# Contiguous 16 KB rows for the experts' down matrices, with a strided channel order in the up products

## The reference

```python
def expert_block(args):
    xb, e = args
    return (jax.nn.silu(xb @ w1[e]) * (xb @ w3[e])) @ w2[e]
```

## Time and profile before

| what | value |
|---|---|
| median of 3 runs | 2577.6 us (2574.97 to 2588.11) |
| the profiled execution | 2590.55 us, span 2588.7 us |
| PE busy | 2180.5 us, 84% of the span |
| VectorE, ScalarE, GpSimd busy | 27%, 18%, 8% |
| queue q1 | 101,632 packets, 496.34 MB, 49.0% of 16 engines over the span |
| queue q0 | 10,880 packets, 16.81 MB, 2.0% |
| packets in all | 112,871, of them 95,344 under 8 KB |
| expert matrices | 192 loads of 2 MB, median 27.5 us from issue to landing |

### The profile page before, as it was taken

The page is one execution under the profiler, slowest core; times in us unless marked ns, Lnnn a source line. Parts: engine busy times, 40 slices in busy tenths (PEclk is TensorE's granted clock), DMA queues, the critical chain, the costliest instruction groups (busy, mean ns, idle before and its releaser), DMA issues.

```text
span 2588.7 us, 32038 instructions
## 1 busy us (share of the span) xinstructions
PE 2180.5 (84%) x13514; PEld 1161.7 (45%) x13514; DVE 689.5 (27%) x1396; ACT 461.7 (18%) x1041; POOL 204.2 (8%) x240
## 2 busy tenths in 40 slices
PE   6899888867999888877778599999999788887773
PEld 3345788864645443222223344775554533222221
DVE  6203667664102221000001321452021310000003
ACT  3211344431102100000000100551021000000001
POOL 1000111101000011111111000000000111111110
PEclk9999899998999889898899799899999799889987
DMA  4020000011224559999998321001324599999994
GB/s 131 33 87 11 10 3 3 3 59 57 98 97 159 204 210 406 406 407 405 407 405 329 136 97 65 33 18 65 130 68 173 229 387 408 408 410 410 401 405 183
DMA packets 112871, 514.96 MB, mean 199 GB/s; under 512 B 20544, under 2 KB 21704, under 8 KB 95344
## 3 DMA queue, kind: packets, MB, share of 16 engines
q1 hardware_dynamic: 101632, 496.34, 49.0%
q0 software_dynamic: 10880, 16.81, 2.0%
q10 hardware_dynamic: 240, 0.07, 0.0%
HBM read 503.73 MB, written 28.31 MB: 206 GB/s over the span
## 4 chain that ended last, share of the span: by engine, by line
PE 64%; DMA 24%; DVE 7%; issue 2%; SPq 2%; ACT 1%; DVEq 0%; POOL 0%; ACTq 0%; POOLq 0%
DMA big<-in_moe_w 23%; PE ps L1510 17%; PE ps L1497 11%; PE ps L1846 8%; PE ps L1616 6%; PE ps L1865 4%; PE ps L1556 2%; PE ps L1717 1%; PE ps L1709 1%; SPq L453 1%; PE ps L1483 1%; PE ps L1770 1%; PE ps L1782 1%; PE ps L1872 1%; PE ps L1731 1%
## 5 line engine op out<-in xcount | busy, mean ns | idle before, releaser
L1846 PE MATMUL ps<-big 128*64 128x512 f32 x2048 | 510.0, 655 | 156.7 <-DMA big<-in_moe_w 156.4
L1510 PE MATMUL ps<-big 128*128 128x512 f32 x1024 | 440.6, 592 | 0.0
L1846 PEld LDWEIGHTS ps<-big 128*64 128x64 f32 x2048 | 176.7, 151 | 486.9 <-issue 486.9
L1510 PEld LDWEIGHTS ps<-big 128*128 128x128 f32 x1024 | 194.3, 190 | 242.7 <-issue 242.5
L1497 PE MATMUL ps<-big 128*128 128x512 f32 (+1 forms) x768 | 277.9, 524 | 6.6 <-issue 6.6
L1426 DVE SCALAR_TENSOR_TENSOR big<-big,ps 128x256 f32<-128x256 f32 x64 | 27.0, 422 | 891.3 <-ACT big L939 891.3
L1865 PE MATMUL ps<-big 128*64 128x512 f32 x1024 | 233.8, 598 | 30.7 <-ACT big L946 30.7
L1497 PEld LDWEIGHTS ps<-big 128*128 128x128 f32 x768 | 146.5, 191 | 136.1 <-issue 128.6
L1616 PE MATMUL ps<-big 64*64 64x64 f32 x5632 | 180.9, 221 | 8.0 <-DVE big L1125 5.5
L1616 PEld LDWEIGHTS ps<-big 64*64 64x64 f32 x5632 | 173.6, 137 | 15.8 <-issue 9.7
L946 ACT ACTIVATE big<-ps 128x256 f32<-128x256 f32 x64 | 24.6, 384 | 677.5 <-PE ps L1855 677.5
(11 more groups left out here) (296 smaller groups left out, 1968.6 us busy)
## 6 DMA issues: line engine op xcount, KB each, us to landing
big<-in_moe_w SPq DMA_DIRECT2D x192, 2048.0 KB, 27.5
big<-in_mx_wkv SPq DMA_DIRECT2D x8, 2048.0 KB, 7.9
big<-in_rw_wrkv SPq DMA_DIRECT2D x6, 2048.0 KB, 8.0
big<-in_mb_wqkv SPq DMA_DIRECT2D x6, 2048.0 KB, 8.0
big<-in_mx_wq SPq DMA_DIRECT2D x4, 2048.0 KB, 8.0
big<-in_mx_wo SPq DMA_DIRECT2D x4, 2048.0 KB, 8.0
h_rows<-big SPq DMA_DIRECT2D x4, 2048.0 KB, 10.3
big<-y_rows SPq DMA_DIRECT2D x8, 1024.0 KB, 8.0
```

The source lines that it names most:

```text
L1510: ins = mm(d[:], lhsT=lhs[:, k, t * P:(t + 1) * P], rhs=w[:, k, :], start=k == 0, stop=k == KT - 1)
L1846: ins = mm(ps[2 + b][half * BR:(half + 1) * BR, :], lhsT=hgT[b][:, k], rhs=w13[set_][:, :, k, half * 256:(half + 1) * 256], start=k == 0, ...
```

## The change

Two lines. The down matrix is now read as `(p k) n`: partition p takes the consecutive rows 4 p to 4 p + 3, one run of 16 KB, as the up matrices do. Group f of `w2` then holds the inner channels 4 p + f rather than 128 f + p. So that the columns of `hT` fit these, the up products take their moving columns in another order. Inner channel 4 q + 2 a + b, with a the half, lands in half a, in column 128 b + q. Within `w13` the neighbours of a moving row are then 4 floats, 16 bytes, apart: 128 of them for b = 0, 128 for b = 1, the same again for the second matrix. The number of instructions, waits and bytes stays on every engine and in every queue, and so does their order.

```diff
             def down_matrix(l, b, e):
-                src = moe_w2[l].rearrange("e (k p) n -> e p k n", p=P)[bass.ds(e, 1)]
+                src = moe_w2[l].rearrange("e (p k) n -> e p k n", p=P)[bass.ds(e, 1)]
                 sp.dma_start(w2[b], src.rearrange("o p k n -> (o p) k n")).then_inc(e_w[l][3 * b + 2], 16)
...
                         for half in range(2):
                             ins = mm(ps[2 + b][half * BR:(half + 1) * BR, :], lhsT=hgT[b][:, k],
-                                     rhs=w13[set_][:, :, k, half * 256:(half + 1) * 256], start=k == 0,
+                                     rhs=w13[set_][:, :, k].rearrange("p s (q a b) -> p s a b q", a=2, b=2)[:, :, half],
+                                     start=k == 0,
                                      stop=k == KT - 1)
```

## The result

The changed kernel takes 2842.93 us (median of 4 runs, 2840.11 to 2845.95) against 2579.42 us before: 1.1002 times as long, 95% interval 1.0972 to 1.1031. It is 264 us slower. The prediction was 20 us faster, with a range from 2529 to 2612 us.

A forecast was written before the change was run, and what follows sets the result against it. The prediction took the expert-matrix transfers to bound the expert stages. 56 down matrices at 0.36 us less each, with strided reads free, gave 20 us less: 2577.6 - 20 = 2557.6 us, range 2529 to 2612.

The forecast's parts named there:

- What bounds the kernel before: Expert stages: transfers set the pace at 15.92 us per block; PE alone needs 12.01, about 3.9 us of room.
- x: What a block's up products gain in length from the strided reads; hidden behind the transfers up to 3.3 us.
- 1300.3 + 31x: Time in us at which PE alone would reach layer 0's last up products; with the transfers these are released at 1403.8.
- I take x = 0: Up products: the strided moving reads were taken to cost PE nothing.
- The sign that the prediction named for this case: Profile after: L1846's mean well above 655 ns with DMA's share falling would show that the stride costs.
- Strided reads cost as VectorE's: Rival, up products: 1.57 times as long, 11.15 us, x = 4.06; 33 us slower, 2611; chance 0.07.
- The two halves stop running side by side: Rival, up products: both streams no longer fit together, x = 6.67; 200 us slower, about 2778; chance 0.16.
- The transfer's gain: Down matrices in 16 KB packets: 0.36 us less each, 56 of them, 20 us less; ends 1 and 49 us.
- 269 extra engine-us: Loaded queue q1: engine time beyond quiet packet prices; put wholly on 4 KB packets, the gain is 0.87 us per matrix.
- quiet packet durations: Preload's quiet stretch: 612 ns per 16 KB packet, 160 ns per 4 KB; 0.23 us less per down matrix.
- fixed overhead per packet: Down matrix transfers: some 3 cycles per packet, by that alone some 0.09 us per matrix and 5 us in all.
- Small effects: Issuing, gathers and scatters, DVE, ScalarE, POOL work and PE's clock: covered or untouched, no cost expected.

The follow-up runs named there:

- experiment 2: Kernel before, but the token-wise projections (L1510, one stream at full width) read their moving operand at a stride of 4 floats: 3059.63 us beside 2579.95.
- experiment 4: Kernel before, but the up products read their moving operand at a stride of 8 floats: 2862.88 us beside 2579.95.
- experiment 3: Kernel before, but only half 0 of each pair of up matmuls reads at a stride of 4 floats, half 1 contiguously: 2869.82 us beside 2579.95.
- experiment 8: Kernel before, but the up matrices come in eight 2 KB rows per partition instead of one of 16 KB: 2638.53 us, ratio 1.0217.

## Why the prediction was wrong

**What bounds the kernel before: right.** 12.01 us per block for PE alone, 15.92 with the transfers. Put in the true x (14.40 less the unhindered 6.87), the prediction's line 1300.3 + 31x gives the result: x = 7.53 makes 1533.7, and the trace after has 1528.63 in an execution that began the stage 5 us earlier.

**"I take x = 0": this is the step that failed.** It rested on two sentences, "an element is wanted only every 0.84 ns per stream" and "VectorE's slow form took a 32-byte step every 1.05 ns, near that pace". PE takes 0.90 us for 512 elements at a stride of 4 floats (experiment 2), 1.76 ns per element, and a row of VectorE did not tell how fast PE fetches: at a stride of 8 floats VectorE took 1.05 ns per element and PE takes 1.79 (experiment 4). The sign that the prediction named for this case came: L1846's mean far above 655 ns, and a DMA share of 0.83 in place of 1.01. All access forms run here fit one rule within 2%: the time is the larger of 0.430 us and 1.76 ns for each 16-byte line touched. A line counts again each time the stream comes back to it from another one, as it does at the strides of 2, 4 and 8.

| moving operand, 512 f32 | lines touched | 1.76 ns each | measured |
|---|---|---|---|
| contiguous | 128 | 0.23 us | 0.430 us |
| stride 2, or pairs | 256 | 0.45 us | 0.450 us |
| stride 3 | 384 | 0.68 us | 0.677 us |
| stride 4 | 512 | 0.90 us | 0.900 us |
| stride 8 | 512 | 0.90 us | 0.918 us |

The measured values are the up products of a block divided by 16, as two of the 32 run side by side (7.20, 10.83, 14.40 and 14.68 us), and L1510's 440.6 / 1024 for the first. The strides of 4 floats gave the figure of 1.76 ns, so that row is no test of it; 2, 3 and 8 are. The line's size was varied only through the stride, never its alignment, so "line" is a reading that fits, not something seen by itself.

The Trainium skill ("SBUF — State Buffer", the note on cachelines in Door 1: The DMA port swizzle) asks for at least two hits per 16-byte line, and these runs agree: 612 ns with two, 1078 with one. Its next sentence, that fp32 may stride by 4 for free, they contradict. I had both sentences ahead of me and no row that decided, and still gave the sign only 0.23.

**The rivals.** "Strided reads cost as VectorE's" came nearest in mechanism (a price of the stride itself, for which no second stream is needed) and had too low a price, up products of 11.15 us where 14.40 came. "The two halves stop running side by side" had nearly the right size, 200 us for 264, and the wrong mechanism: experiments 2 and 3 show that each stream pays alone, and a lone full-width stream pays too. Its x of 6.67 was too low by 0.86 us, which over 31 blocks and both layers is 53 of the 64 us between them. Of this, 0.22 us is a slip that all its x share: they were counted from 7.09 us, but the 12.01 us of an unhindered block go with 6.87. The range ended at 2612 because I left this case out.

**The transfer's gain: right sign, too large.** 0.36 us per down matrix was taken, 0.12 measured. The failing term is the share of the 269 extra engine-us that was put on small packets: with large packets there were 288, so they did not go with small ones. What they go with is not shown. Of the remaining 0.23 us from the quiet packet durations only half arrived, which fits the share over 100% of the 4 KB packets in the earlier trace rows: their times overlap, so their sum is too large a price. The Trainium skill's fixed overhead per packet ("DMA: Bandwidth & Descriptors", Why small descriptors are slow (HBM only)) gave an estimate of 5 us, and the 6 us measured (2 to 11) agree with it. By these 3 cycles alone, on 64 beats, the 2 KB rows of experiment 8 would cost some 23 us, an estimate; measured were 56.

**Small effects: right.** In the chain of the changed kernel SyncE's issues and GpSimd stand at 0% of the span and all transfers at 1%, and VectorE and ScalarE at 6% and 2% where they had 7% and 1%.

## What to carry to other kernels

A longer DMA row bought by a stride on the moving operand is a trade between two engines, and the stride is the dearer side: with f32 at a stride of at most 2 floats, or with neighbours kept in pairs, the price is 5% of the matmul instead of 110%. If an order has to be changed, look for the smallest operand on the way (here the 128 x 256 gated rows, once per block) and change it there. When a cost has no row in the trace and two readings of a rule disagree, let the range reach to the worse one.

## What was not expected of the hardware

Making one of the two streams contiguous gains nothing: 14.50 us of up products per block, as with both strided (experiment 3), since each strided instruction keeps its length and they follow one another. A weight load with a stride of 2 floats takes 206 ns at the median instead of 140, while the moving operand at the same stride loses only 20 ns of 592. The strided f32 read costs PE 1.76 ns per element, and VectorE's whole instruction, at a stride of 8 floats, takes 1.05 ns per element.
